# Attention over 16 heads of 64 channels: q and k copied to the opposite partitions, each head's scores split over the two halves of TensorE's rows, and a postponed normalisation cut into three pieces

## What is computed

```python
q = apply_rope(q.reshape(B, S, N_ATT_HEADS, HEAD_DIM), pos) * (HEAD_DIM ** -0.5)
k = apply_rope(k.reshape(B, S, N_ATT_HEADS, HEAD_DIM), pos)
...
s = jnp.einsum('bdhnqc,bdhnkc->bdhnqk', qb, kw)      # causal, three dilation patterns
p = jnp.exp(s - m)
o = jnp.einsum('bdhnqk,bdhnkc->bdhnqc', p, vw) / den[..., None]
...
att = dilated_mixture_attention(q, k, v, pos) * jax.nn.silu(z_att)
...
y = ((y - mean) * lax.rsqrt(var + LNX_EPS)).reshape(B, S, R) * lnx_g + lnx_b
return (y + bonus) * g * jax.nn.silu(z)              # the recurrence's output
...
x = x + jnp.matmul(jnp.concatenate([att, rwk], axis=-1), w_out)
return rms_norm(x, final_g)
```

## Time and profile before

| | |
|---|---|
| median of 3 executions | 3190.18 us (3187.8 to 3192.78) |
| the profiled execution, its own time | 3181.01 us |
| its span, first to last instruction | 3179.2 us |
| PE busy | 3042.0 us (96%) |
| POOL, DVE, ACT busy | 1653.8, 1331.1, 1142.5 us |
| mean granted TensorE clock | 0.985 |
| attention stage | from 2896 to 3000 us of the span |

### The profile page before, as it was taken

The page is one execution under the profiler, slowest core; times in us unless marked ns, Lnnn a source line. Parts: engine busy times, 40 slices in busy tenths (PEclk is TensorE's granted clock), DMA queues, the critical chain, the costliest instruction groups (busy, mean ns, idle before and its releaser), DMA issues.

```text
span 3179.2 us, 53119 instructions
## 1 busy us (share of the span) xinstructions
PE 3042.0 (96%) x21132; PEld 2393.6 (75%) x21132; DVE 1331.1 (42%) x2083; ACT 1142.5 (36%) x1523; POOL 1653.8 (52%) x1360
## 2 busy tenths in 40 slices
PE   7899999999899999999999989999999999998997
PEld 5677778878688888888877857777777777775675
DVE  8789862110423132231322053454454454455612
ACT  4355543233433232332323243233233233234521
POOL 5556544444677777777753424353343343344242
PEclk9999999999999999999999999999999999998998
DMA  4576674232122222222222232222222222224522
GB/s 165 164 204 181 190 194 157 92 137 102 66 87 99 82 95 86 90 95 85 97 83 79 93 128 96 88 83 89 87 83 89 87 83 89 87 72 141 170 93 92
DMA packets 126976, 348.13 MB, mean 110 GB/s; under 512 B 59872, under 2 KB 62944, under 8 KB 96240
## 3 DMA queue, kind: packets, MB, share of 16 engines
q1 hardware_dynamic: 126832, 346.00, 33.0%
HBM read 306.33 MB, written 34.90 MB: 107 GB/s over the span
## 4 chain that ended last, share of the span: by engine, by line
PE 70%; issue 10%; POOL 9%; DVE 6%; ACT 3%; SPq 1%; DMA 1%; POOLq 0%; DVEq 0%; ACTq 0%
PE bank L184 20%; PE bank L186 19%; PE bank L185 19%; POOL wlo L167 8%; PE bank L1165 1%; PE bank L1183 1%; ACT whi L162 1%; PE bank L1836 1%; PE bank L1523 1%; PE bank L1534 1%; DVE g L1360 1%; PE bank L1174 1%; PE bank L1502 0%; PE bank L1910 0%; PE bank L1876 0%
## 5 line engine op out<-in xcount | busy, mean ns | idle before, releaser
L167 POOL TENSOR_TENSOR wlo<-wraw,whi 128x512 fp32r<-128x512 f32 (+1 forms) x916 | 1226.9, 1369 | 1296.6 <-ACT whi L162 1296.4
L184 PE MATMUL bank<-rhi,whi 128*128 128x512 f32 x3648 | 1486.3, 407 | 77.0 <-POOL wlo L167 42.3
L185 PE MATMUL bank<-rlo,whi 128*128 128x512 f32 x3648 | 1428.3, 392 | 0.0
L186 PE MATMUL bank<-rhi,wlo 128*128 128x512 f32 x3648 | 1428.1, 391 | 0.0
L184 PEld LDWEIGHTS bank<-rhi,whi 128*128 128x128 f32 x3648 | 688.3, 189 | 270.9 <-issue 54.3
L185 PEld LDWEIGHTS bank<-rlo,whi 128*128 128x128 f32 x3648 | 689.5, 189 | 146.7 <-issue 15.3
L186 PEld LDWEIGHTS bank<-rhi,wlo 128*128 128x128 f32 x3648 | 688.4, 189 | 147.2
L162 ACT ACTIVATE whi<-wraw 128x2048 fp32r<-128x2048 f32 (+2 forms) x232 | 438.3, 1889 | 542.9 <-PE bank L186 345.8
L993 POOL TENSOR_TENSOR wraw<-wraw,vec 128x512 f32<-128x512 f32 x260 | 266.6, 1056 | 0.0
L897 DVE TENSOR_TENSOR ssum<-ssum,wk 128x512 f32<-128x512 f32 x30 | 21.6, 720 | 314.4 <-ACT wk L887 314.4
L887 ACT ACTIVATE wk<-bank 128x512 f32<-128x512 f32 x32 | 27.9, 872 | 239.1 <-PE bank L186 239.1
(11 more groups left out here) (351 smaller groups left out, 2952.6 us busy)
## 6 DMA issues: line engine op xcount, KB each, us to landing
wraw<-in_wall_dram SPq DMA_DIRECT2D x224, 1024.0 KB, 4.9
g<-in_bmat_dram SPq DMA_DIRECT2D x16, 512.0 KB, 4.0
g<-scr_e SPq DMA_DIRECT2D x128, 64.0 KB, 3.1
scr_a<-ssum SPq DMA_DIRECT2D x24, 256.0 KB, 2.3
g<-in_xp_dram SPq DMA_DIRECT2D x4, 1024.0 KB, 10.4
g<-in_cmat_dram SPq DMA_DIRECT2D x16, 256.0 KB, 7.2
scr_u<-wk SPq DMA_DIRECT2D x16, 256.0 KB, 2.4
scr_y<-wk SPq DMA_DIRECT2D x16, 256.0 KB, 3.2
```

What stands on the lines that cost most here:

```text
L167: ins = pool.tensor_tensor(wlo[:, slot, c], wraw[:, slot, c], whi[:, slot, c].bitcast(F32), ALU.subtract)
L184: pe.matmul(acc[slot][:, :], whk, rhi[:, k, :], start=(k == first), stop=False)
L185: pe.matmul(acc[slot][:, :], whk, rlo[:, k, :], start=False, stop=False)
L186: ins = pe.matmul(acc[slot][:, :], wlk, rhi[:, k, :], start=False, stop=(k == last))
```

## The change

1. **Stores.** `aside_store` writes the sine parts of q and k with the blocks of 32 already exchanged, as four DMAs of 32 partitions each. A pass raises `a_wr` by 192 where it was 96. `at_load` then reads both sine parts in one DMA.
2. **Doubling.** When POOL has formed q and k (`a_qk`), a new `at_double(p)` copies them, SBUF to SBUF, into `sw0` or `sw1` with the two halves of the partitions exchanged: two DMAs of 64 partitions by 1024 elements. The semaphore `a_du` counts them, and PE waits for it ahead of the first head of each pair.
3. **Scores.** Blocks b = 3 and 0 use q and k as before, and b = 2 and 1 use the copy on the other 64 partitions, so on the other half of PE's rows. b = 0 moves to the bank of b = 2 and waits until two of the head's matmuls are done. The minima for b = 2 wait for all four.
4. **SP's list.** `at_double` is put in for each pair. The load of the gate of pair 1, which waits for `rw_out`, moves behind `at_load(3)` and ahead of `at_double(3)`.
5. **Norm of the last pass.** `rw_root` moves from behind head 0 to behind head 2, and `rw_norm` is cut in three parts, behind heads 3, 4 and 5.
6. **Inputs of the last product.** ACT's `w2_hi` and POOL's `w2_lo` for blocks 7 on come later, two at a time in places.

```diff
@@ aside, aside_store
-            d.wait_ge(a_wr, 96 * p + (16, 48, 80, 112)[i])
+            d.wait_ge(a_wr, 192 * p + (16, 96, 176, 208)[i])
...
             if i < 2:
-                sp.dma_start(scr_a[p, 3 + i], xt["zt2"]).then_inc(a_wr, 16)
+                for q in range(4):
+                    to, of = 32 * q, 32 * (q ^ 1)
+                    sp.dma_start(scr_a[p, 3 + i, to:to + 32], xt["zt2"][of:of + 32, :]).then_inc(a_wr, 16)
@@ rw_norm (in the other passes its three parts run one behind the other)
+        def rw_norm(d, link, p, part):
             cn = w["lc"]
+            if part == 0:
+                link(d.tensor_tensor(cn, cn, w["t2"], ALU.mult))
+                link(d.tensor_scalar(cn, cn, vcol(V_LG, p), vcol(V_LB, p), ALU.mult, ALU.add))
+            elif part == 1:
+                d.wait_ge(rw_bn, p + 1)
+                link(d.tensor_tensor(cn, cn, w["bonus"], ALU.add))
+                link(d.tensor_tensor(cn, cn, w["g"], ALU.mult))
+            else:
+                d.wait_ge(rw_zs, p + 1)
+                d.tensor_tensor(col(g2, p + 8), cn, w["zs"], ALU.mult).then_inc(rw_out, 1)
@@ attention stage
-        as_at = [(1, 384), (1, 0), (2, 0), (0, 0)]
+        as_at = [(2, 384), (1, 0), (2, 0), (0, 0)]
@@ at_load
-            for i in range(4):
-                to, of = 32 * i, 32 * (i ^ 1)
-                sp.dma_start(at[f"sw{u}"][to:to + 32, :].rearrange("p (i t) -> p i t", i=2),
-                             scr_a[p, 3:5, of:of + 32].rearrange("i p t -> p i t")).then_inc(a_ld[u], 16)
+            sp.dma_start(at[f"sw{u}"].rearrange("p (i t) -> p i t", i=2), scr_a[p, 3:5].rearrange("i p t -> p i t"))\
+              .then_inc(a_ld[u], 16)
+        def at_double(sp, p):
+            u = p % 2
+            sp.wait_ge(a_qk, p + 1)
+            for hd in range(2):
+                sp.dma_start(at[f"sw{u}"][hs_[hd], :], at[f"in{u}"][hs_[1 - hd], 0:2 * T]).then_inc(a_du[u], 16)
@@ at_scores
             if hd == 0:
                 pe.wait_ge(a_qk, p + 1)
+                pe.wait_ge(a_du[u], 32 * (p // 2) + 96)
...
+                if b == 0:
+                    pe.wait_ge(a_s, 4 * h + 2)
                 to = ab_[hd][bank][:, o:o + n]
-                pe.matmul(to, at_q[u][hs_[hd], b * P:(b + 1) * P], at_k[u][hs_[hd], 0:n], start=True, stop=True)\
+                q_, k_, rows = (at_q[u], at_k[u], hs_[hd]) if b in (0, 3) else \
+                    (at[f"sw{u}"][:, 0:T], at[f"sw{u}"][:, T:2 * T], hs_[1 - hd])
+                pe.matmul(to, q_[rows, b * P:(b + 1) * P], k_[rows, 0:n], start=True, stop=True)\
                   .then_inc(a_s, 1)
@@ at_minima
-                d.wait_ge(a_s, 4 * h + (4 - b if b >= 2 else 4))
+                d.wait_ge(a_s, 4 * h + (2 if b == 3 else 4))
@@ at_dve
                 if h == 0:
                     xb_add(d, 3)
+                if h == 2:
                     rw_root(d, link, 7)
-                if h == 1:
-                    rw_norm(d, link, 7)
+                if 3 <= h <= 5:
+                    rw_norm(d, link, 7, h - 3)
@@ at_act
-                if h == 3:
-                    w2_hi(act, range(NBK, 8))
-                if h % 2 and h >= 5:
-                    w2_hi(act, range((h - 5) // 2 + 8, (h - 5) // 2 + 9))
+                if h % 2 and h >= 7:
+                    w2_hi(act, {7: range(7, 9), 9: range(9, 11), 11: range(11, 12), 13: range(12, 13), 15: range(13, 14)}[h])
@@ at_pool
-                if p >= 2:
-                    w2_lo(pool, range(p + 5, p + 6))
+                if p >= 4:
+                    w2_lo(pool, (range(7, 9), range(9, 10), range(10, 12), range(12, 13))[p - 4])
@@ at_sp
             at_load(sp, 1)
+            at_double(sp, 0)
             xb_store(sp, 1)
...
+            at_double(sp, 1)
+            for p in range(2, 8):
                 at_load(sp, p)
-                at_load_z(sp, p - 1)
+                if p == 3:
+                    sp.wait_ge(rw_out, 8)
+                    at_load_z(sp, 1)
+                if p >= 3:
+                    at_load_z(sp, p - 1)
+                at_double(sp, p)
```

More of the change, by code:

```diff
@@ L1440, in rw_dve @@
             rw_root(d, link, p)
-            rw_norm(d, link, p)
+            for part in range(3):
+                rw_norm(d, link, p, part)
             rw_inputs(d, link, p + 1, 1)
@@ L1448, in rw_root @@
             link(d.reciprocal(w["t2"], w["t2"]))
-        def rw_norm(d, link, p):
+        def rw_norm(d, link, p, part):
             cn = w["lc"]
-            link(d.tensor_tensor(cn, cn, w["t2"], ALU.mult))
-            link(d.tensor_scalar(cn, cn, vcol(V_LG, p), vcol(V_LB, p), ALU.mult, ALU.add))
-            d.wait_ge(rw_bn, p + 1)
-            link(d.tensor_tensor(cn, cn, w["bonus"], ALU.add))
-            link(d.tensor_tensor(cn, cn, w["g"], ALU.mult))
-            d.wait_ge(rw_zs, p + 1)
-            d.tensor_tensor(col(g2, p + 8), cn, w["zs"], ALU.mult).then_inc(rw_out, 1)
+            if part == 0:
[8 more added lines that the diff above has]
+                d.tensor_tensor(col(g2, p + 8), cn, w["zs"], ALU.mult).then_inc(rw_out, 1)
         def rw_pe(pe, p, nxt):
@@ L1804, in at_load @@
               .then_inc(a_ld[u], 16)
-            for i in range(4):
-                to, of = 32 * i, 32 * (i ^ 1)
-                sp.dma_start(at[f"sw{u}"][to:to + 32, :].rearrange("p (i t) -> p i t", i=2),
-                             scr_a[p, 3:5, of:of + 32].rearrange("i p t -> p i t")).then_inc(a_ld[u], 16)
+            sp.dma_start(at[f"sw{u}"].rearrange("p (i t) -> p i t", i=2), scr_a[p, 3:5].rearrange("i p t -> p i t"))\
+              .then_inc(a_ld[u], 16)
+        a_du = [y_in[2], y_in[3]]
+        def at_double(sp, p):
[3 more added lines that the diff above has]
+                sp.dma_start(at[f"sw{u}"][hs_[hd], :], at[f"in{u}"][hs_[1 - hd], 0:2 * T]).then_inc(a_du[u], 16)
         def at_load_z(sp, p):
@@ L1817, in at_turn @@
             u = p % 2
-            pool.wait_ge(a_ld[u], 80 * (p // 2) + 80)
+            pool.wait_ge(a_ld[u], 32 * (p // 2) + 32)
             qk = at[f"in{u}"][:, 0:2 * T]
@@ L1999, in at_pool @@
                     make_lo(pool, N_W2 + p - 1, p - 1)
-                if p >= 2:
-                    w2_lo(pool, range(p + 5, p + 6))
+                if p >= 4:
+                    w2_lo(pool, (range(7, 9), range(9, 10), range(10, 12), range(12, 13))[p - 4])
             w2_lo(pool, range(13, 14))
         def at_sp(sp):
-            sp.wait_ge(a_wr, 16 + 96 * 8)
+            sp.wait_ge(a_wr, 16 + 192 * 8)
             xb_load(sp, 0)
@@ L2022, in at_sp @@
                 w_load_next(sp, N_W2 + i, i)
-            sp.wait_ge(a_wr, 16 + 96 * 8 + 16)
-            at_load(sp, 2)
-            sp.wait_ge(rw_out, 8)
-            at_load_z(sp, 1)
-            for p in range(3, 8):
-                at_load(sp, p)
-                at_load_z(sp, p - 1)
+            sp.wait_ge(a_wr, 16 + 192 * 8 + 16)
+            at_double(sp, 1)
+            for p in range(2, 8):
+                at_load(sp, p)
+                if p == 3:
[4 more added lines that the diff above has]
+                at_double(sp, p)
             at_load_z(sp, 7)
```

## The result

The changed kernel takes 3201.13 us and the kernel before 3189.20, medians of 13 executions each. The ratio is 1.0039 (95% interval 1.0028 to 1.0049): slower by about 12 us.

The account below looks back on a forecast made before the run. It took DVE and ACT to set the steady pairs at 9.65 us, with the start mattering most. +5.8 us for the start and -3.4 for heads 8 to 15 gave +2.4 on 3190.18: 3192.6 us, range 3183 to 3202.

Parts of the forecast that it names:

- The ring rival: Pairs 4 to 7: load, turn and copy take 13.2 to 14.7 us against 13.2 available; +9, 3199 us; chance 15%.
- stores in the recurrence: Six more store issues a pass on SP's queue, 2.4 us a pass, were to cost 0.
- S(0): S(h) is the start of head h's first minimum on DVE; S(0) was forecast at 2899.7, 2.5 us late.
- X, on before's scale: X is the end of the last pass's norm, when rw_out rises; forecast 2940.2, bounds 2937 and 2943.
- heads 8 to 15: Fewer transpose waits (0.7), less DVE-POOL lock (1.5), PE's sooner end (1.2): -3.4 us including head 15's end.
- The stall at head 6: DVE stops 5 us or more for PE, which waits for pair 3's copy, then half clock; S(6) = X + 6.8.
- The copy of pair 1 is issued at 2905.7 behind two weight loads and a store, 5.2 to landing: Ahead of head 2: copy lands at 2910.9, PE restarts at half clock, S(2) = 2912.9 where it was 2918.06.
- I take X + 4.9: Head 6: pair 3's copy lands 4.9 us after the norm's end X, bounds X + 4.1 and X + 6.
- Scores of a warm head in about 1.3 us: PE's scores at full clock: 640 columns a half, 1.2 us, about 1.3 with the wait ahead of b = 0.
- The copies didn't come early: Rival of early copies: X = 2937.5, S(8) = 2952.3, about -7, 3183 us; chance 15%.
- the halves do work side by side: Rival that they don't: waits of heads 8 to 15 stay, three cold scores cost 2 more each; +9, 3199 us; 6%.
- cold from the start: Rival: PE at half clock after waiting 2.4 us at head 0, slowing projection and head 1; +8, 3198 us; 12%.

Follow-up runs that it names:

- e3: Changed kernel without the copies, blocks 2 and 1 reading the other head's q and k (values not the reference's): 3182.78 us, 0.9988 to before.
- e8: Changed kernel, copies and split kept, norm one head earlier, copies of pairs 1 and 3 issued sooner on SP: 3190.87 us, 1.0010 to before.
- e7: Changed kernel without copies and split, norm one head earlier, pair 1's gate load behind pair 3's load: 3178.92 us, 0.9978 to before.
- e11: As e7, but blocks 2 and 1 read the other head's rows without a copy (values not the reference's): 3178.63 us, 0.9963 to before.
- e9: As e8, with the copies of pairs 2 to 7 issued from ACT's queue: 3189.21 us, 1.0006 to before.
- e13: As e8, with only the copies of pairs 5 to 7 issued from ACT's queue: 3189.63 us, 1.0002 to before.
- e1: Changed kernel with pair 3's copy issued ahead of the wait for rw_out and the gate loads: 3194.33 us, 1.0019 to before.

## Why the prediction was off

The number, 3192.6 us, was 8.5 us low, outside the forecast's own range (3188 to 3197) and inside the range given (3183 to 3202). It is inside by 0.9 us, through an upper end that was put there for the rivals, so its fit is luck in part. The sum had +2.4 us where the medians differ by 11.9. The case that came is the ring's in its effect. Each term, with what it measured in the differences of S - t0:

| term | predicted | measured |
|---|---|---|
| stores in the recurrence | 0 | 0: 119.2 us a pass in before and after |
| S(0) | +2.5 | +2.2 |
| S(2) | -5.2 | -1.8 |
| X, on before's scale | 2940.2 | 2943.7 |
| X to PE's restart, S(6), S(8) | 4.9, 6.8, 18.6 | 6.3, 8.5, 19.0 |
| S(8) | +5.8 | +9.7 |
| heads 8 to 15 | -2.2 | +4.5 |
| the end behind S(15) | -1.2 | -1.4 |
| sum | +2.4 | +12.8 |

**The bound and the sign of the start: right.** DVE and ACT set a pair at 9.65 us (e3), and the start is where the change loses. The stall at head 6 came as described: DVE stopped for PE, PE for `g<-g`, half clock (0.50) behind it. S(0), and S(1) with it (2905.1 on before's scale, as forecast), are right.

**The step "The copy of pair 1 is issued at 2905.7 behind two weight loads and a store, 5.2 to landing": off by 3.2 us.** It was issued when I said (2914.76 - 9.1), but PE restarted 8.4 us behind the issue, and S(2) was 3.4 late. Each of its two DMAs took 6.8 us. From 2915 to 2924 the SP queue's share of the 16 DMA engines was (packets, MB, share)

```profile
q1 hardware_dynamic: 1043, 2.55, 99.3%
```

I had counted what stands ahead of the copy, two weight loads and a store, and not what SP issues right behind it: the load of pair 2, 1.28 MB, from 2915.96, which landed 8.0 and 9.3 us later. That the two shared the engines is read from this share; no run took the load away alone. The 3.2 us that the prediction worked out for 512 KB come near where no large transfer is beside the copy (3.5), and not here. All the difference in X (3.5) is this, handed on through heads 2 to 5 without loss or gain. So S(8) was late by 3.5 for X and 0.4 for the rest.

**The step "I take X + 4.9": off by 1.4,** and beyond its bound of X + 6. Four issues took 1.97 us where I had 1.6, and the last DMA 4.4 us where my upper bound was that too. It hardly counted: S(8) came at X + 19.0, as the cold heads 6 and 7 were cheaper than forecast.

**The term "Heads 8 to 15 ... Sum: -3.4": the step that failed.** I let `turn` move "to about S + 1" because scores end sooner. It came at S + 3.2 in pair 5 and still beside the scaling. The load of pair p + 1 stands behind the copy of pair p, which waits for the turn of pair p: that order was in the list of SP in the prediction's own front, and I costed only the load's condition on the scores. The ring rival had the effect (+9) at 15%, but by another mechanism: it reckoned the time from scores to scores as a deadline of the load, and put the loss at pairs 4 to 7 through that. What sets the pace is the queue's order, 11 to 12 us a round (e8). The runs without this order take less for heads 8 to 15: 35.6 us with the copies and the split out (e7), 34.6 with only the copies out (e11), 35.6 with the copies in another queue (e9).

On DVE the loss hardly shows as a wait for a copy: 0.19 us at S(10), none at S(12). It shows as work beside POOL, 5.4 us of longer scalings for before's 3.7. The turns fall 2.5 to 3.2 us behind S, where before had them at 1.8 to 2.2, and two of them meet the second scaling of a head, behind which DVE has no wait for ACT that would hide it. In e9 and e7, without the ring, this is 2.5 and 2.4 us, in e8 over 6. How much of the 4.5 us is the ring's pace and how much the scalings' wasn't separated. The prediction had named both signs of being wrong: `turn` beside the scaling as often as before, and PE waiting for the copies of later pairs.

**What the ring doesn't explain.** S(8) to S(15) cost 4.5 us. The rounds, 11.0 to 11.5 us for 10.3, account for some 3, an estimate. The remainder fits the stretch at half clock, some 6 us from 3000 on, in which the values took 4.14 us for 2.38 and DVE waited 1.44 and 0.50 us behind them; no run took that alone away.

**"Scores of a warm head in about 1.3 us": 1.68.** It is the wait ahead of b = 0 that I had at 0.1. In PE's timeline of after the second pass of b = 3 starts at 2928.94, and b = 0 at 2929.63:

```profile
2928.94 1.18 PE L1853 MATMUL bank<-g 64*128 64x512 f32 x5
...
2929.63 0.48 PE L1853 MATMUL bank<-g 64*128 64x128 f32 x2
```

With everything in a row the next matmul starts 0.43 us behind the second pass (a 512-column matmul, 2 passes, then occupies 2 x 0.43 and 0.1 at its start). Here it is 0.69: b = 0 waits until two of the head's matmuls are done, of which b = 3, on the same half of the rows, is the later, 0.26 us, and begins with a pass that is 0.1 longer. Together 0.36, and 1.68 less 0.36 is the 1.3 of the estimate. In odd heads the 2.00 us have another cause: in e11 b = 2 starts 0.54 us behind b = 3 there, and 0.01 in even heads. It didn't set the time, since PE was no longer the bound.

**The rivals.** The copies didn't come early, the halves do work side by side (e11), and PE stayed at full clock behind the 2.12 us at head 0 (1.00 in the window above), so it wasn't cold from the start.

**What stays open.** Why a cold head after the stall was cheaper than reckoned was not followed up. Whether a copy issued from ACT ahead of the next load would be free wasn't tried; e9 and e13 both had it behind.

## What to carry over

A DMA that waits for a computation holds up everything behind it in its queue, so when one is put in, follow the ring that it closes (issue, landing, engine, next issue) and set its length against the time of a pair, before anything else is costed. A faster engine is worth what its inputs' new traffic leaves: here the split gave 6.9 us and its copies took 11.7 by the profiles, and the medians show the second alone (15). And a semaphore that is raised later, as `rw_out`, delays each transfer queued behind its wait, which shows one stage at a time: remove the first stall and the next comes up (e1, from head 6 to head 8).
